# Forget-gate mixer: four heads' squares added on GpSimd, one product with ones instead of four, one stretch of fillers later

## The reference, cut to what matters

```python
o_hg, S1_hg = hgrn_scan(heads(silu(hg_q)), heads(k_hg), heads(hg_i), heads(log(g_f)), S0_hg)
y_hg = rmsnorm(unheads(o_hg), p['hg_norm_w']) * silu(hg_g)
# rmsnorm: x * rsqrt(mean(x * x, -1) + EPS) * w, the mean over all 4 heads x 128 = 512 features
```

## Time and profile before

| | us |
|---|---|
| median of three runs | 2128.03 |
| the profiled execution, its own time | 2125.46 |
| its span, first to last instruction | 2123.7 |
| PE busy in the span | 2086.6 (98%) |
| DVE busy | 1181.1 (56%) |
| ACT busy | 887.4 (42%) |
| POOL busy | 953.0 (45%) |

### The profile page before, as it was taken

The page is one execution under the profiler, slowest core; times in us unless marked ns, Lnnn a source line. Parts: engine busy times, 40 slices in busy tenths (PEclk is TensorE's granted clock), DMA queues, the critical chain, the costliest instruction groups (busy, mean ns, idle before and its releaser), DMA issues.

```text
span 2123.7 us, 39063 instructions
## 1 busy us (share of the span) xinstructions
PE 2086.6 (98%) x14550; PEld 2022.6 (95%) x14550; DVE 1181.1 (56%) x1875; ACT 887.4 (42%) x1688; POOL 953.0 (45%) x736
## 2 busy tenths in 40 slices
PE   7999999999999999999999999999999999999997
PEld 6999999999899999899999899999999999999996
DVE  5788423232756555234445456567554458766665
ACT  5555333233355555133333233335444445444434
POOL 2338723232212111312212222218767677988886
PEclk9999999999999999999999999999999999999999
DMA  4224546442344332355643454323434447544422
GB/s 176 74 69 130 168 134 190 124 137 73 102 130 137 102 108 72 112 192 148 197 132 108 136 190 147 126 91 126 158 138 147 155 162 265 163 140 146 134 91 87
DMA packets 229926, 287.66 MB, mean 135 GB/s; under 512 B 42190, under 2 KB 163570, under 8 KB 229670
## 3 DMA queue, kind: packets, MB, share of 16 engines
q1 hardware_dynamic: 202700, 244.70, 36.8%
q10 hardware_dynamic: 27098, 41.23, 5.4%
HBM read 194.66 MB, written 91.21 MB: 135 GB/s over the span
## 4 chain that ended last, share of the span: by engine, by line
PE 81%; POOL 7%; DVE 4%; ACT 3%; issue 2%; DMA 2%; SPq 0%; ACTq 0%; DVEq 0%; POOLq 0%
PE D L451 40%; PE PB L3005 26%; PE MM L1321 2%; POOL b_u L754 1%; POOL b_t L757 1%; POOL w_lo L431 1%; POOL ring_lo L2943 1%; DVE u_x L565 1%; DMA w_raw<-in_w_half 1%; PE MM L891 1%; POOL w_lo L2943 1%; PE MM L1919 1%; POOL lw_lo L2943 1%; PE MB L1315 0%; DMA f_rs<-hd 0%
## 5 line engine op out<-in xcount | busy, mean ns | idle before, releaser
L451 PE MATMUL D<-xn_hi,w_hi 128*128 128x352 f32 x1992 | 663.1, 333 | 3.5 <-DVE acc L2798 2.1
L451 PE MATMUL D<-xn_lo,w_hi 128*128 128x352 f32 x1992 | 643.4, 323 | 0.0
L451 PE MATMUL D<-xn_hi,w_lo 128*128 128x352 f32 x1992 | 643.1, 323 | 0.0
L431 POOL TENSOR_TENSOR w_lo<-w_raw,w_hi 128x1024 fp32r<-128x1024 f32 (+1 forms) x105 | 242.3, 2308 | 803.4 <-ACT w_hi L425 803.4
L451 PEld LDWEIGHTS D<-xn_hi,w_hi 128*128 128x128 f32 x1992 | 374.9, 188 | 18.8 <-issue 12.8
L451 PEld LDWEIGHTS D<-xn_lo,w_hi 128*128 128x128 f32 x1992 | 374.7, 188 | 4.7 <-issue 3.8
L451 PEld LDWEIGHTS D<-xn_hi,w_lo 128*128 128x128 f32 x1992 | 374.8, 188 | 0.0
L3005 PE MATMUL PB<-x_hi,w_hi 128*128 128x264 f32 x876 | 250.7, 286 | 4.9 <-ACT stage L3041 2.8
L3005 PE MATMUL PB<-x_hi,w_lo 128*128 128x264 f32 x876 | 250.3, 286 | 0.0
L3005 PE MATMUL PB<-x_lo,w_hi 128*128 128x264 f32 x876 | 250.1, 285 | 0.0
L3005 PE MATMUL PB<-x_lo,ring_hi 128*128 128x264 f32 x860 | 244.9, 285 | 0.0
(11 more groups left out here) (594 smaller groups left out, 3782.8 us busy)
## 6 DMA issues: line engine op xcount, KB each, us to landing
w_raw<-in_w_proj SPq DMA_DIRECT2D x73, 512.0 KB, 3.8
proj<-stage ACTq DMA_DIRECT2D x60, 528.0 KB, 3.1
hd<-stage SPq DMA_DIRECT2D x64, 264.0 KB, 2.5
f_rs<-hd SPq DMA_DIRECT2D x50, 264.0 KB, 2.8
stage<-hd SPq DMA_DIRECT2D x48, 264.0 KB, 2.8
w_raw<-in_w_full SPq DMA_DIRECT2D x24, 512.0 KB, 4.3
stage<-proj SPq DMA_DIRECT2D x23, 528.0 KB, 3.5
hd<-f_rs SPq DMA_DIRECT2D x32, 264.0 KB, 2.1
```

Of the source, the lines that this page charges most:

```text
L431: nc.gpsimd.tensor_tensor(w_lo[t.slot][:, 0:kt, :], raw(t)[0][:, 0:kt * P].rearrange("p (k m) -> p k m", m=P), w_hi[t.slot][:, 0:kt, :].bi ...
L451: last = nc.tensor.matmul(D[b][:, 0:GN], w[t.slot][:, k, :], x, start=(k == 0 and n == 0), stop=(k == kt - 1 and n == 2))
```

## The change

The four products with `ones` per prompt chunk become one. POOL adds in place: first heads 0,1 plus heads 2,3 (128x256), then the rest (128x128). POOL does this after its slot 0 and before its slot 1, in which it calls L431. PE's sum moves behind slot 2 and waits for POOL's second addition instead of ACT's square. The sample tokens keep the four products. The semaphore `hg_levels`, which nobody waits for, gets another name.

```diff
-        hg_pool = steps("hg_pool", "gw", credit=1)
+        hg_pool = steps("hg_pool", "gw s0 s1", credit=1)
...
             if kind == "pool":
...
-                    for _ in range(6):
+                    slot()
+                    eng.wait_ge(*act_.after("sq", n))
+                    for k in range(2):
+                        half_ = C4 >> (k + 1)
+                        if k:
+                            eng.wait_ge(*pool_.after("s0", n))
+                        eng.tensor_tensor(g_y[:, 0:half_], g_y[:, 0:half_], g_y[:, half_:2 * half_], ALU.add).then_inc(*pool_.step(f"s{k}"))
+                    for _ in range(5):
                         slot()
             if kind == "pe":
...
                 slot()
-                eng.wait_ge(*act_.after("sq", n))
-                for h in range(H):
-                    i = eng.matmul(M[3][:, 0:N], ones, g_y[:, h * N:(h + 1) * N], start=(h == 0), stop=(h == H - 1))
+                if sample:
+                    eng.wait_ge(*act_.after("sq"))
+                else:
+                    slot()
+                    eng.wait_ge(*pool_.after("s1", n))
+                for h in range(H if sample else 1):
+                    i = eng.matmul(M[3][:, 0:N], ones, g_y[:, h * N:(h + 1) * N], start=(h == 0), stop=(not sample or h == H - 1))
                 i.then_inc(*pe_.step("ss"))
...
                 else:
-                    for _ in range(5):
+                    for _ in range(4):
                         slot()
```

More of the change, by code:

```diff
@@ L823, in build @@
         hg_dve = steps("hg_dve", "at cp0 cp1 cp2 cp3 s1 s2 y1 y2", credit=1)
-        hg_pool = steps("hg_pool", "gw", credit=1)
-        hg_v, hg_levels = sem("hg_v"), sem("hg_levels")
+        hg_pool = steps("hg_pool", "gw s0 s1", credit=1)
+        hg_v, begun = sem("hg_v"), sem("begun")
         hg_out = sem("hg_out")
@@ L1222, in hgrn @@
                     eng.wait_ge(*dve_.after("at", n))
-                    eng.sem_inc(hg_levels, 1)
+                    eng.sem_inc(begun, 1)
                     eng.copy_predicated(g_at[:, :].rearrange("p (a h b c) -> p a h b c", a=2, h=2, c=2)[:, :, :, :, 1],
```

## The result

| | before | after |
|---|---|---|
| median, us (runs) | 2127.98 (6) | 2136.56 (6) |
| lowest to highest | 2127.14 to 2130.16 | 2134.26 to 2144.18 |
| the profiled execution, its own time | 2125.46 | 2144.18 |
| its span | 2123.7 | 2142.4 |

The changed kernel takes 1.0047 of the time of the one before (95% interval 1.0037 to 1.0056): slower by 8.6 us in the medians, where 1.2 less was forecast.

The account below looks back on a forecast made before the run. PE, busy 98%, bounds the kernel; seven chunks gain 0.28 - 0.2 = 0.08 us (0.56) and the last 0.67, together 1.2: 2128.03 - 1.2 = 2126.8 us. Own range 2124.5 to 2128.5, whole range 2122.5 to 2131.5.

Parts of the forecast that it names:

- PE's new wait: At PE's sum behind slot 2: POOL's additions end by 707.1, at most 709.1, before PE comes at 710.07; costs nothing.
- Rival 4: At PE's sum: POOL is shut out until PE waits for the second addition, some 0.5 us a chunk; 2128 to 2130; chance 0.06.
- The room before the bank: Before PE's slot 4, which needs the bank ACT copies group 1 from: 0.28 us between release and PE's start.
- d: How much later POOL's additions make DVE's `dk1`, on which ACT's copy and PE's slot 4 hang: taken as 0.2 us.
- rival 1: Strict turns at the DVE/POOL port: additions go straight into DVE's subtractions, d = 0.75; +2.6 us, 2130.6; chance 0.17.
- its likeliest case: The forecast itself, in the mixer's chunks: d between -0.1 and 0.4, own range 2124.5 to 2128.5 us; chance 0.46.
- The six passes: In PE's sum of squares: six of eight passes go, 0.111 us each, 0.67 us a chunk, 5.3 us in eight.
- DMAs and the SP queue don't change: On the DMA and SP queues: the change was taken to leave them as they are, with no cost counted.

Follow-up runs that it names:

- e1: Changed kernel with POOL's two additions ahead of L431 instead of behind it, PE's wait kept: 2132.04 us, ratio 1.0028 to the kernel before.
- e5: e1 plus ACT copying group 1 ahead of the next chunk's key exponentials: 2139.72 us, ratio 1.0059 to the kernel before.
- e3: Kernel before with one product behind slot 2, first head's squares only, three heads left out, no additions: 2126.24 us, ratio 0.9995.
- e9: e5 plus SP issuing the next chunk's input loads ahead of the weight load: 2121.23 us, ratio 0.9973 to the kernel before.
- e6: e3 plus ACT copying group 1 ahead of the key exponentials: 2125.10 us, ratio 0.9990 to the kernel before.
- e8: Changed kernel, additions still behind L431, plus ACT's early copy of group 1: 2136.47 us, ratio 1.0042 to the kernel before.
- e2: Kernel before with all four products moved behind slot 2, waiting for ACT's square alone, no additions: 2127.18 us, ratio 1.0001.

## Why the prediction was wrong

**PE's new wait: the step that failed.** The prediction has "so the first addition is issued near 705.87" and, of the end of both additions before PE comes, "this wait costs nothing". The step took the additions to be issued as soon as the square was ready, ahead of L431. In the diff two calls of `slot()` stand ahead of POOL's wait for the square, the common one and the added one, and the second is the slot in which POOL makes `w_lo`. The additions had to be put behind L431, whose row was at hand (2.65 us, 3.98 in the second chunk). In the times of the earlier trace rows: L431 ends at 706.81 + 2.65 = 709.46, two additions of 1.52 us in all (as measured) end at 710.98, PE comes at 710.07, so a stop costs 0.9 us; with L431 at 3.98 and the additions at 1.76 it costs 2.5. Less the 0.16 of overlap those are the idle times found, 0.77 and 2.3. The sentence under "The change" that places the additions before POOL's slot 1 carries the same misreading: they stand behind it, before slot 2. e1 has the order that the prediction assumed, and PE does not wait for POOL in it.

**Rival 4's wait is what happened, by another mechanism and at another price.** It had PE waiting for the second addition, but through a lost turn at the port, 0.5 us a chunk, 2128 to 2130, at a chance of 0.06. Measured: 0.8 us in four chunks and 2.3 in four. The measured 2136.56 lies outside the whole range given, whose upper end is 2131.5. How many chunks would be of the long kind was not to be had from the trace of before, where one in eight was.

**The low clock was in none of the cases.** The trace of before has none in the mixer, and no stop there. But it has one at another place, where PE stops for 2.06 us (the window's columns as in the earlier trace rows):

```profile
1468.17 0.56 PE L3005 MATMUL PB<-x_hi,w_hi 128*128 128x264 f32 x1 [2.06 <-ACT stage L3041]
...
1468.13:1471.54 3.41, 3.37 (x15) 3.40 (x16) 1.58 (x2) 1.88 (x6) 3.41 (x3) 0.50 0.49 183
```

So a rival with stops of 2 us and more could have been given this price as well: up to 1.7 us on top of the stop, half of 3.41, and up to 3.4 once in e5, where the low stretch lasted 6.83.

**The room before the bank.** The mechanism stands (in e1 and e3 all of PE's waits in the mixer are for L470), the size was off: 0.28 us forecast, 0.11 measured. The release was read off a product behind ACT's L1180 as 0.05; for the copy it is 0.14 to 0.15 (e1, e3), and a restart costs 0.08 that the prediction didn't count; 0.28 - 0.10 - 0.08 = 0.10.

**d.** Forecast 0.2, measured 0.84 in the order that was assumed (e1). The second addition does get its turn, and so does L431 behind it. With this and the room of 0.11, rival 1's sum comes to 7 x 0.73 - 0.67 = +4.4, where it had +2.6; e1 has +5.6 in the medians. So even for a kernel with the order that the prediction assumed its likeliest case was too low, by d and the room: the weight given to the rows in which L431 lost its turn was wrong for operations issued back to back.

The Trainium skill ("SBUF — State Buffer", section "Who interferes with whom") says that whoever issues first keeps the shared port for the whole instruction. The seven chunks of e1 agree, with the subtractions stretched from 4.62 to 5.46 us each time. The 3.96 us of L431 in after agree only in part: it was issued at 603.25, within the run of seven subtractions, and stood through the rest of the run and L1248 before it got the port.

What decides which kind a chunk becomes is in part in the traces. The eleven kernels in which L431 is not behind the additions have 77 such L431 (first seven chunks each). In 28 of them a subtraction had just started, 0 to 12 ns before L431, and all 28 are of the short kind. In the other 49 the next subtraction started 1 to 35 ns after L431; all 18 of the long kind are among these, with 31 short ones. In before one of seven chunks was issued in this second way, and became long; in after six of seven, and four became long. Why some of these lose and some don't stays open.

**The six passes.** 0.111 us each, 0.67 a chunk: right (0.68 in e9).

**That DMAs and the SP queue don't change: wrong at second hand.** In e5 SP's order was worth more than the whole change, because L1150 stands behind a load that waits for L431. In e6, where nobody adds, it cost 2.5 us.

So the change asks for time on four queues at once, and each had less slack than the 0.67 us that PE gains: POOL (additions behind L431), the shared port (0.8 us), ACT (copy behind keys, 0.11 us), SP (inputs behind a weight load). Once three of them are put in order (e9), the gain is there.

## What to carry to other kernels

Before a wait is costed at nothing, write down the queue of the engine that is to release it, instruction by instruction, with the calls of helpers counted; "idle for 17 us" says nothing about what stands ahead of the new work. On a kernel that is bound by one engine, a saving on it is only worth the smallest slack among the queues that feed it, so read the slack of each (bank, masks, loads, weights) and move the cheap ones forward with the saving. Price a stop of PE at its idle time, a restart, and half of the low-clock stretch that may follow it.

## What the runs showed of the hardware

- In the 14 traces PE stops 28 times for 2.06 to 3.20 us (between 40 and 2105 us), and with 22 of these comes a stretch at the granted clock 0.5, which begins within the stop or up to 1.6 us behind it and lasts 3.41 us (once 6.83). In after these are three of four stops of 2.3 us in the mixer, in e8 one of two, in e5 all three of 3.1 to 3.2. Of 111 stops of 0.65 to 1.82 us none has one, the seven of 1.13 to 1.17 in e1 and the four of 0.8 in after among them. In e2 and in after a stretch came in the sample tokens with no stop over 0.15 us before it.
- POOL's L431 issued in DVE's run of subtractions: 3.96 to 3.99 us where it was shut out, 2.56 to 2.70 where it had the next turn; with DVE elsewhere 2.4. It was shut out in none to four of seven chunks, by the kernel. Where the two additions came just ahead of it in the run, it never was (e1, e9).
- POOL's addition of 128x256 and of 128x128 together: 1.50 to 1.58 us where they took turns with DVE's subtractions or followed L431's short form, 1.76 to 1.79 behind the long form, 1.3 in after's last chunk; e5, where DVE's work lies otherwise, has 1.38 and 2.08 once each.
- A release from ACT's copy reached PE after 0.14 to 0.15 us, one from POOL's addition after 0.05 to 0.06. A stop costs, besides its idle time, 0.16 us of overlap with the matmul before and some 0.1 at the restart.
